# A hybrid NSA and Mamba2 block in float32: in the MLP, another order of the tiles in the first quad of each down projection, and the last split of squared rows one slot later

## The chip, the cores and the metric

The kernel runs on one core of one Trainium2 chip. The metric is the device time of one execution in microseconds (us), lower is better. The times of the kernel before are three runs; one more execution was recorded by the hardware profiler, and all rows and durations below come from that one.

## The reference, cut to what matters

One layer of a decoder block on 256 tokens of width 2048, all in float32: an RMSNorm, one wide input projection, two token mixers (sparse attention and a Mamba2 scan), gated and merged, an output projection, and then the MLP, which the change touches:

```python
h = h + merged @ w_out[l]
hn = rms_norm(h, norm_mlp_w[l])
h = h + jnp.square(jax.nn.relu(hn @ w_up[l])) @ w_down[l]      # w_up 2048 x 8192, w_down 8192 x 2048
return rms_norm(h, norm_final_w)
```

## The kernel before, in words

**One tile of weights.** All weights stream from HBM in tiles of 128 x 2 x 512 float32 (512 KB): two rows of blocks k = 2j and 2j + 1 of 512 columns. A tile takes four steps on four engines. SP loads it into one of four buffers `raw` (L674 in the MLP). ACT copies it, rounded, into one of four buffers `hi` (L1545, or L1541 for a tile of sums). DVE writes the remainder `lo = raw - hi` (L2132). PE multiplies the stationary activations, which are also kept as a high and a low part (`LAh`, `LAl`), with it: three matmuls of 512 columns for each product (high x high, high x low, low x high). Each engine has a program of its own in one common order of tiles, and they meet in counting semaphores: `s_lo` for `lo` tiles made, `s_mm` for tiles multiplied, `s_raw` for landings. Three limits follow. ACT may write `hi` of a tile only when PE is done with the tile four before. SP may load into a buffer only when DVE has made `lo` of the tile that was in it, which is four loads before. DVE and ACT work LEAD = 3 tiles ahead of the tile that PE is at: slot s of their program handles tile s + 3 of the phase and then runs the further work that is hooked to slot s.

**The MLP** has four phases, one for each 2048 of the 8192 hidden columns. A phase first makes its part of `hn @ w_up` in 4 chunks of 8 tiles (UP = 32 tiles), then multiplies the squared result with `w_down`, in two quads (QUAD = 22 tiles each, columns 0 to 1023 and 1024 to 2047). In the last phase the second quad is 16 plain tiles (TWO_ORDER) instead.

**The squared rows.** After chunk k of the up part is multiplied, slot 8k + 7 takes it out of PSUM (ACT L1527 and DVE L2100 with relu, ACT L1532 squares), DVE turns blocks of 32 x 32 (L423), and POOL spreads these over the partitions with four DMAs (L432, 128 KB each). Slot 8k + 11 then makes the stationary operands for k-blocks 4k to 4k + 3 of the down part: `LAh` on ACT (`act_split_s`, L447), which waits for the DMAs, and `LAl` on DVE (`dve_split_s`, L457), which waits for `LAh`. For k = 3 that is slot 35, when DVE has passed tile 38. PE needs these last rows only from the tile ("n", 0, 6) on.

**A quad** makes the output blocks of two column chunks for both halves of the tokens. Ten tiles are plain ("n"): j = 3 to 7 for each of the two chunks, 12 matmuls each. For j = 0 to 2 the kernel uses a scheme of seven block products in place of eight (`seven_products`), as four tiles each:

- a: weights of chunk 0, 6 matmuls. DVE first forms sums `TQ[0]` out of the raw tiles of a and b (L2122), so it waits until both have landed, then makes `lo`.
- b: weights of chunk 1, 3 matmuls. DVE forms `TQ[1]` in two steps with a drain between (L2126, L2128), then half a tile of `lo` (128 x 512).
- p and q: no load. ACT and DVE split `TQ[0]` and `TQ[1]`, 6 matmuls each.

The raw buffer of a is free again only when b's `lo` is made. So the load that goes into a's buffer and the one that goes into b's are both issued at that moment, four loads on. The order of the 22 tiles is QUAD_ORDER. `tiles_of_phase` turns it into the table that SP, ACT and DVE follow, and `four_blocks` on PE walks it too. In the words below a0, b0, p0, q0 are the tiles of j = 0, and n03 is ("n", 0, 3).

Of the kernel before, what the change touches and what calls it, by code (L numbers as in the profile page):

```python
# [76 lines left out]
G_MLP = 8 * C_MLP  # L77
G_END = G_MLP + 3 * PHASE + UP + QUAD + TWO

QUAD_ORDER = ([("n", 0, j) for j in (3, 4, 5)] + [("n", 1, 3)] + [(c, 0, 0) for c in "abpq"] +  # L80
              [("n", 1, j) for j in (4, 5)] + [(c, 0, 1) for c in "abpq"] + [("n", 0, j) for j in (6, 7)] +
              [(c, 0, 2) for c in "abpq"] + [("n", 1, j) for j in (6, 7)])
TWO_ORDER = [("n", c, j) for c in range(2) for j in range(8)]


def tiles_of_phase(last):

    tiles, loads = [("n", x // 8, x % 8, x) for x in range(UP)], UP
    for q in range(2):
        for kind, c, j in (TWO_ORDER if last and q else QUAD_ORDER):  # L90
            tiles.append((kind, 4 + 2 * q + (c if kind == "n" else 0), j, loads))
            loads += kind not in "pq"
    return tiles
# [25 lines left out]
def build(nc, a, out):  # L119
    ctx = ExitStack()  # L120
    with ctx:
# [16 lines left out]
        LAh = sb("LAh", [P, KT, S], F32R)  # L138
        LAl = sb("LAl", [P, KT, S], F32R)
# [303 lines left out]
        def act_split_s(act, n, Lh, k0, wc=None, later=0):  # L443

            act.wait_ge(s_sp[n % 2], 64 * (n // 2 + 1) + later)
            if wc is None:
                x = act.activation(tokens(Lh, k0), spread(n), ACT.Copy)  # L447
            else:
                for ct in range(4):
                    x = act.activation(tokens(Lh, k0 + ct, 1), spread(n, ct), ACT.Copy, scale=wc[:, ct:ct + 1])  # L450
            x.then_inc(s_tra, 2)

        def dve_split_s(dve, n, e, Lh, Ll, k0, wc=None):

            dve.wait_ge(s_tra, 2 * e + 2)
            if wc is None:
                x = dve.tensor_tensor(tokens(Ll, k0), spread(n), tokens(Lh, k0).bitcast(F32), ALU.subtract)  # L457
            else:
                for ct in range(4):
                    for t in range(2):  # L460
                        x = dve.scalar_tensor_tensor(tokens(Ll, k0 + ct, 1)[:, t, :, :], spread(n, ct)[:, t, :, :], wc[:, ct:ct + 1],
                                                     tokens(Lh, k0 + ct, 1)[:, t, :, :].bitcast(F32), ALU.mult, ALU.subtract)
            x.then_inc(s_trd, 1)
# [419 lines left out]
        def _(pe):  # L883
# [140 lines left out]
            for i in range(0, NG):  # L1024
                C, e = C_AT + 4 * i, E_AT + PER_AT * i
# [169 lines left out]
            def four_blocks(i, q):  # L1195

                g, C = G_MLP + PHASE * i + UP + QUAD * q, C_MLP + 8 * i + 4 + 2 * q
                p0, p1 = C % 2, (C + 1) % 2
                pe.wait_ge(s_acc, C - 1)
                for y, (kind, c, j) in enumerate(QUAD_ORDER):  # L1200
                    if kind == "a":
                        if j == 0:
                            pe.wait_ge(s_sfl, 2 * i + 2)
                            if 2 * i + q:
                                pe.wait_ge(s_ux, 2 * i + q)
                        seven_products(g + y, j, p0, p1)
                    elif kind == "n":
                        if c == 0 and j == 6:
                            pe.wait_ge(s_trd, E_MLP + 4 * i + 4)
                        if (c, j) == (1, 3):  # L1210
                            pe.wait_ge(s_acc, C)
                        mlp_group(g + y, (p0, p1)[c], j, LAh, LAl, t_first=(j == 3, j == 3), last=((c, j) == (1, 7)))
# [26 lines left out]
        def _(act):  # L1239
# [171 lines left out]
            for i in range(NG):  # L1411
                C, e = C_AT + 4 * i, E_AT + PER_AT * i
                hk, late = late, {}
# [11 lines left out]
                for r in range(4):  # L1425
                    n, s0 = 4 * i + r, SL_S[i][r]
# [81 lines left out]
            hk = scan_hooks(7, 12)  # L1508
# [67 lines left out]
            def mlp(i, first=False):  # L1576
                g, e = G_MLP + PHASE * i, E_MLP + 4 * i
                hk = {}
                for k in range(4):
                    hk[8 * k + 7] = [lambda k=k: first_rows(g + 8 * k + 8, (C_MLP + k) % 2), lambda k=k: square_rows(4 * i + k)]  # L1580
                    hk[8 * k + 11] = [lambda k=k: act_split_s(act, 8 + k, LAh, 4 * k, later=128 * i)]
                hk[14] = [lambda: row_sums(i)]
                hk[22] = [lambda: third_row_sums(i)]
                for q in range(1 if i == LAST else 2):
                    hk[UP + QUAD * q + 19] = [lambda q=q: copy_first(2 * i + q, g + UP + QUAD * q + 20)]
                if i == LAST:
                    hk[UP + QUAD + 3] = [lambda: act.wait_ge(s_hq, 7), lambda: residual_squares(C_END - 4, 0)]
                    hk[UP + QUAD + 4] = [lambda: act.wait_ge(s_ss, SS_WO + 2), lambda: residual_squares(C_END - 3, 1)]
                    hk[UP + QUAD + 7] = [lambda: act.wait_ge(s_ss, SS_WO + 4), lambda: residual_squares(C_END - 2, 2)]
                if first:  # L1590
                    hk[4] = [lambda: act_split_s(act, 7, LBh, 12, COLS[:, CN2 + 12:CN2 + 16])]
                phase_slots(i, hk)
# [22 lines left out]
        def _(dve):  # L1615
# [299 lines left out]
            for i in range(NG):  # L1915
                C, e = C_AT + 4 * i, E_AT + PER_AT * i
                hk, late = late, {}
# [14 lines left out]
                for r in range(4):  # L1932
                    n, s0 = 4 * i + r, SL_S[i][r]
# [14 lines left out]
            for i in range(2):  # L1948
                C = C_PA + 2 * i
                hk = {} if i else late  # L1950
# [107 lines left out]
            hk = scan_hooks(7, 12)  # L2058
# [165 lines left out]
            def mlp(i, before, first=False):  # L2224
                C, g, e = C_MLP + 8 * i, G_MLP + PHASE * i, E_MLP + 4 * i
                hk, late = before, {}
                for k in range(4):
                    hk[8 * k + 7] = [lambda k=k: mlp_rows(k, 4 * i + k, (C_MLP + k) % 2, XA_UP + 4 * i + k + 1)]
                    hk[8 * k + 11] = [lambda k=k: dve_split_s(dve, k, e + k, LAh, LAl, 4 * k)]
                hk[13] = [lambda: row_sums(i)]  # L2230
                hk[15] = hk.get(15, []) + [lambda: row_sums_low(i)]
                hk[21] = [third_row_sums]
                hk[24] = [lambda: third_row_sums_low(i)]
                quad_hooks(hk, late, i, 0)
                if i == LAST:
                    hk[UP + QUAD + 3] = [lambda: weigh(0), lambda: weigh(1)]
                    hk[UP + QUAD + 7] = [lambda: add_blocks(G_END - 8, C_END - 2, 2), lambda: weigh(2)]
                else:
                    quad_hooks(hk, late, i, 1)
                if first:  # L2240
                    hk[4] = [lambda: dve_split_s(dve, 7, E_WO + 3, LBh, LBl, 12, COLS[:, CN2 + 12:CN2 + 16])]
                phase_slots(i, hk)
                return late
# [62 lines left out]
```

## Time and profile before

| | |
|---|---|
| three runs | 2026.34 us median (2026.10 to 2029.11) |
| profiled execution, its own time | 2029.81 us |
| its span in the profile | 2028.1 us |
| PE busy | 2008.5 us, 99% |
| DVE, ACT, POOL busy | 1501.5 (74%), 1095.9 (54%), 277.9 us (14%) |
| share of the chain that ended last | PE 86%, DVE 6%, ACT 2%, DMA 2% |
| traffic | 203 GB/s mean |

The profile is one execution. Its busy times say how much of the span an engine worked, its rows of waits say how long an engine stood and for whom, and its timelines give the start of each instruction. "PEld" is the load of stationary weights, which overlaps the matmuls. A matmul's end is modelled, so of PE it is the starts that are read.

### The profile page before, as it was taken

How to read it: one execution, taken by the hardware profiler on the slowest of the kernel's cores; microseconds unless marked ns; L12 is line 12 of the kernel's file. 1: busy time of each engine (PE TensorE's matmuls, PEld its weight loads, DVE VectorE, ACT ScalarE, POOL GpSimd, SP SyncE). 2: the span in 40 equal slices, each digit the busy share in tenths (PEclk: the TensorE clock that was granted, in tenths of full speed). 3: DMA queues.
4: the chain of work that ended last, by engine and by line, in shares of the span. 5: the costliest groups of instructions: out<-in, count | busy, mean ns of one | idle time of the engine just before them, and what ended most of it. 6: DMA issues, size and time to landing. Idle time of an engine off the chain costs nothing.

```text
span 2028.1 us, 25969 instructions
## 1 busy us (share of the span) xinstructions
PE 2008.5 (99%) x9330; PEld 1655.7 (82%) x9330; DVE 1501.5 (74%) x1923; ACT 1095.9 (54%) x1533; POOL 277.9 (14%) x415
## 2 busy tenths in 40 slices
PE   9999999999999999999999999999999999999998
PEld 7888888888888888788888788888888888878886
DVE  5766868777765688886678877766886797697686
ACT  5444555555553576674567644555555554555554
POOL 4001111111010133331033310110000000100000
PEclk9999999999999999999999999999999999999999
DMA  8757666666657666666666677676666666666764
GB/s 259 222 173 216 194 190 197 189 196 191 183 181 229 186 193 191 195 195 209 177 186 197 192 237 244 215 222 216 199 210 215 197 211 203 215 200 203 230 206 150
DMA packets 203018, 411.52 MB, mean 203 GB/s; under 512 B 15296, under 2 KB 15648, under 8 KB 201488
## 3 DMA queue, kind: packets, MB, share of 16 engines
q1 hardware_dynamic: 188944, 364.75, 57.9%
q0 software_dynamic: 13776, 44.96, 7.7%
q8 instruction: 74, 1.21, 0.2%
q14 instruction: 48, 0.39, 0.1%
q10 hardware_dynamic: 176, 0.20, 0.0%
HBM read 379.91 MB, written 2.16 MB: 188 GB/s over the span
## 4 chain that ended last, share of the span: by engine, by line
PE 86%; DVE 6%; ACT 2%; DMA 2%; issue 1%; DVEq 1%; POOL 0%; ACTq 0%; POOLq 0%
PE acc L349 18%; PE acc L351 17%; PE acc L350 17%; PE acc L1155 8%; PE acc L1157 8%; PE acc L1156 8%; DVE lo L2132 2%; DVE lo L313 1%; DMA XTOK<-W 1%; PE x L1066 1%; PE tr L1015 1%; DMA raw<-w_in 1%; PE tr L384 1%; PE x L998 1%; ACT hi L307 1%
## 5 line engine op out<-in xcount | busy, mean ns | idle before, releaser
L313 DVE TENSOR_TENSOR lo<-raw,hi 128x1024 fp32r<-128x1024 f32 x434 | 532.2, 1240 | 267.5 <-ACT hi L307 260.9
L307 ACT ACTIVATE hi<-raw 128x1024 fp32r<-128x1024 f32 x434 | 452.1, 1057 | 329.8 <-PE acc L351 272.6
L349 PE MATMUL acc<-hi,LAh 128*128 128x512 f32 x1344 | 535.3, 398 | 3.2 <-DVE lo L313 2.8
L351 PE MATMUL acc<-hi,LAl 128*128 128x512 f32 x1344 | 524.3, 390 | 0.0
L350 PE MATMUL acc<-lo,LAh 128*128 128x512 f32 x1344 | 523.5, 390 | 0.0
L1545 ACT ACTIVATE hi<-raw 128x1024 fp32r<-128x1024 f32 x253 | 253.2, 1020 | 153.1 <-PE acc L1157 119.8
L2132 DVE TENSOR_TENSOR lo<-raw,hi 128x1024 fp32r<-128x1024 f32 x253 | 292.1, 1176 | 54.5 <-ACT hi L1545 51.6
L349 PEld LDWEIGHTS acc<-hi,LAh 128*128 128x128 f32 x1344 | 252.3, 188 | 58.8 <-issue 7.6
L351 PEld LDWEIGHTS acc<-hi,LAl 128*128 128x128 f32 x1344 | 252.2, 188 | 54.1
L350 PEld LDWEIGHTS acc<-lo,LAh 128*128 128x128 f32 x1344 | 252.5, 188 | 51.2 <-issue 1.4
L1155 PE MATMUL acc<-hi,LBh 128*128 128x512 f32 x512 | 199.2, 389 | 0.0
L1156 PE MATMUL acc<-lo,LBh 128*128 128x512 f32 x512 | 199.2, 389 | 0.0
L1157 PE MATMUL acc<-hi,LBl 128*128 128x512 f32 x512 | 199.2, 389 | 0.0
L349 PE MATMUL acc<-hi,LBh 128*128 128x512 f32 x384 | 150.4, 392 | 0.0
L351 PE MATMUL acc<-hi,LBl 128*128 128x512 f32 x384 | 149.5, 389 | 0.0
L350 PE MATMUL acc<-lo,LBh 128*128 128x512 f32 x384 | 149.4, 389 | 0.0
L1155 PE MATMUL acc<-hi,LAh 128*128 128x512 f32 x328 | 127.6, 389 | 0.0
L1156 PE MATMUL acc<-lo,LAh 128*128 128x512 f32 x328 | 127.6, 389 | 0.0
L1157 PE MATMUL acc<-hi,LAl 128*128 128x512 f32 x328 | 127.6, 389 | 0.0
L1157 PEld LDWEIGHTS acc<-hi,LBl 128*128 128x128 f32 x512 | 96.1, 188 | 20.1
L1156 PEld LDWEIGHTS acc<-lo,LBh 128*128 128x128 f32 x512 | 96.1, 188 | 20.0
L1155 PEld LDWEIGHTS acc<-hi,LBh 128*128 128x128 f32 x512 | 96.1, 188 | 19.7
(423 smaller groups left out, 2475.0 us busy)
## 6 DMA issues: line engine op xcount, KB each, us to landing
raw<-w_in SPq DMA_DIRECT2D x304, 512.0 KB, 4.3
raw<-w_up SPq DMA_DIRECT2D x128, 512.0 KB, 4.1
raw<-w_down SPq DMA_DIRECT2D x128, 512.0 KB, 4.9
raw<-w_proj_ssm SPq DMA_DIRECT2D x64, 512.0 KB, 4.4
raw<-w_proj_nsa SPq DMA_DIRECT2D x32, 512.0 KB, 4.7
raw<-w_out SPq DMA_DIRECT2D x32, 512.0 KB, 5.4
W<-acs_rows POOLq DMA_DIRECT2D x8, 1024.0 KB, 6.6
W<-TB POOLq DMA_DIRECT2D x48, 128.0 KB, 4.3
```

The costliest lines, as they stand in the source:

```text
L307: act.activation(hi[:, sl, :, :], raw[:, sl, :, :], ACT.Copy).then_inc(s_hi, 1)
L313: dve.tensor_tensor(lo[:, sl, :, :], raw[:, sl, :, :], hi[:, sl, :, :].bitcast(F32), ALU.subtract).then_inc(s_lo, 1)
L349: pe.matmul(o, xh, wh, start=(k == 0), stop=False)
L350: pe.matmul(o, xh, wl, start=False, stop=False)
L351: x = pe.matmul(o, xl, wh, start=False, stop=(k == KT - 1))
L384: x = pe.transpose((banks or TR)[b][:, (ct % 2) * S + t * P:(ct % 2) * S + (t + 1) * P], src[:, t, ct * P:(ct + 1) * P], identf[:, :])
L998: pe.matmul(X6[:, :], Q[:, n, P:S], K[:, :, 0:2 * P].rearrange("p k (b n) -> p b k n", b=2), start=(p_ == 0), stop=(p_ == 2), skip_group_c ...
L1155: pe.matmul(o, xh, wh, start=(kk == 0 and t_first[t]), stop=False)
L1156: pe.matmul(o, xh, wl, start=False, stop=False)
L1157: x = pe.matmul(o, xl, wh, start=False, stop=(last and kk == 1))
L1545: act.activation(hi[:, sl, k0:2, :], raw[:, d % RING, k0:2, :], ACT.Copy).then_inc(s_hi, 1)
L2132: dve.tensor_tensor(lo[:, sl, k0:2, :], src, hi[:, sl, k0:2, :].bitcast(F32), ALU.subtract).then_inc(s_lo, 1)
```

## The change

The first quad of every phase gets an order of its own: six plain tiles first instead of four, and one plain tile between the groups of four instead of two. The second quad keeps its order. The last split of squared rows (k = 3) moves from slot 35 to slot 36 on ACT and on DVE, in all four phases.

```diff
-QUAD_ORDER = ([("n", 0, j) for j in (3, 4, 5)] + [("n", 1, 3)] + [(c, 0, 0) for c in "abpq"] +
-              [("n", 1, j) for j in (4, 5)] + [(c, 0, 1) for c in "abpq"] + [("n", 0, j) for j in (6, 7)] +
-              [(c, 0, 2) for c in "abpq"] + [("n", 1, j) for j in (6, 7)])
+QUAD_ORDER = (([("n", c, j) for c in range(2) for j in (3, 4, 5)] + [(c, 0, 0) for c in "abpq"] + [("n", 0, 6)] +
+               [(c, 0, 1) for c in "abpq"] + [("n", 0, 7)] + [(c, 0, 2) for c in "abpq"] + [("n", 1, j) for j in (6, 7)]),
+              ([("n", 0, j) for j in (3, 4, 5)] + [("n", 1, 3)] + [(c, 0, 0) for c in "abpq"] +
+               [("n", 1, j) for j in (4, 5)] + [(c, 0, 1) for c in "abpq"] + [("n", 0, j) for j in (6, 7)] +
+               [(c, 0, 2) for c in "abpq"] + [("n", 1, j) for j in (6, 7)]))
...
-        for kind, c, j in (TWO_ORDER if last and q else QUAD_ORDER):
+        for kind, c, j in (TWO_ORDER if last and q else QUAD_ORDER[q]):
...
-                for y, (kind, c, j) in enumerate(QUAD_ORDER):
+                for y, (kind, c, j) in enumerate(QUAD_ORDER[q]):
...
-                    hk[8 * k + 11] = [lambda k=k: act_split_s(act, 8 + k, LAh, 4 * k, later=128 * i)]
+                    hk[8 * k + 11 + k // 3] = [lambda k=k: act_split_s(act, 8 + k, LAh, 4 * k, later=128 * i)]
...
-                    hk[8 * k + 11] = [lambda k=k: dve_split_s(dve, k, e + k, LAh, LAl, 4 * k)]
+                    hk[8 * k + 11 + k // 3] = [lambda k=k: dve_split_s(dve, k, e + k, LAh, LAl, 4 * k)]
```

On DVE, in the first phase, from the take of the last up chunk (`XR<-acc`) through the first group of four to the second. Before (the rows `lo<-TQ` are p and q, `lo<-raw` of 128x512 is b):

```order
L2100 TENSOR_SCALAR XR<-acc,RS 128x512
L423 STREAM_TRANSPOSE W<-Y 128x4x4x32 x2
L2132 TENSOR_TENSOR lo<-raw,hi 128x1024
L2122 TENSOR_TENSOR TQ<-raw 128x1024
L2132 TENSOR_TENSOR lo<-raw,hi 128x1024
L2126 TENSOR_TENSOR TQ<-TQ,raw 128x512
L2128 TENSOR_TENSOR TQ<-raw,TQ 128x512
L2132 TENSOR_TENSOR lo<-raw,hi 128x512
L2132 TENSOR_TENSOR lo<-TQ,hi 128x1024
L457 TENSOR_TENSOR LAl<-XTOK,LAh 128x1024
L2132 TENSOR_TENSOR lo<-TQ,hi 128x1024
L2132 TENSOR_TENSOR lo<-raw,hi 128x1024 x2
```

The same place with the change (line numbers are two higher):

```order
L2102 TENSOR_SCALAR XR<-acc,RS 128x512
L425 STREAM_TRANSPOSE W<-Y 128x4x4x32 x2
L2134 TENSOR_TENSOR lo<-raw,hi 128x1024 x3
L2124 TENSOR_TENSOR TQ<-raw 128x1024
L2134 TENSOR_TENSOR lo<-raw,hi 128x1024
L2128 TENSOR_TENSOR TQ<-TQ,raw 128x512
L2130 TENSOR_TENSOR TQ<-raw,TQ 128x512
L2134 TENSOR_TENSOR lo<-raw,hi 128x512
L459 TENSOR_TENSOR LAl<-XTOK,LAh 128x1024
L2134 TENSOR_TENSOR lo<-TQ,hi 128x1024 x2
L2134 TENSOR_TENSOR lo<-raw,hi 128x1024
```

Two plain tiles have moved ahead of the first sums, `LAl` stands before both p0 and q0 instead of between them, and one plain tile is left before the next sums. On ACT, at the same place, before:

```order
L1532 ACTIVATE Y<-XR 128x1024
L1545 ACTIVATE hi<-raw 128x1024 x2
L1545 ACTIVATE hi<-raw 128x512
L1541 ACTIVATE hi<-TQ 128x1024
L447 ACTIVATE LAh<-XTOK 128x1024
L1541 ACTIVATE hi<-TQ 128x1024
L1545 ACTIVATE hi<-raw 128x1024 x3
```

and with the change:

```order
L1534 ACTIVATE Y<-XR 128x1024
L1547 ACTIVATE hi<-raw 128x1024 x4
L1547 ACTIVATE hi<-raw 128x512
L449 ACTIVATE LAh<-XTOK 128x1024
L1543 ACTIVATE hi<-TQ 128x1024 x2
L1547 ACTIVATE hi<-raw 128x1024 x2
```

`LAh` now stands before both high parts of the sums. No instruction is added or removed on any engine.

## Rows read from the trace of the kernel before

**Rows 1.** The page, parts 1 and 6: busy times and loads.
```profile
PE 2008.5 (99%) x9330; PEld 1655.7 (82%) x9330; DVE 1501.5 (74%) x1923; ACT 1095.9 (54%) x1533; POOL 277.9 (14%) x415
...
raw<-w_down SPq DMA_DIRECT2D x128, 512.0 KB, 4.9
```

**Rows 2.** Waits of PE and PEld: total us, times, longest us.
```profile
PE tr L1170 <- DVE lo L2132: 3.9, 4, 1.2
...
PEld x L1170 <- DVE lo L2132: 1.7, 3, 0.6
```

**Rows 3.** Timeline of PE, first phase: start us, us, engine, line.
```profile
1417.91 0.39 PE L1155 MATMUL acc<-hi,LAh 128*128 128x512 f32 x1
...
1420.63 0.39 PE L1155 MATMUL acc<-hi,LAh 128*128 128x512 f32 x1
...
1431.96 0.39 PE L1172 MATMUL x<-hi,LSl 128*128 128x512 f32 x1
1433.51 0.50 PE L1170 MATMUL tr<-hi,LSh 128*128 128x512 f32 x1 [1.16 <-DVE lo L2132]
1433.85 0.40 PE L1171 MATMUL tr<-lo,LSh 128*128 128x512 f32 x1
```

**Rows 4.** Timeline of ACT, first quad of the first phase.
```profile
1430.00 1.06 ACT L447 ACTIVATE LAh<-XTOK 128x1024 fp32r<-128x1024 f32 x1 [2.67 <-DMA XTOK<-W]
```

**Rows 5.** Timeline of DVE, first quad of the first phase.
```profile
1422.80 1.18 DVE L2132 TENSOR_TENSOR lo<-raw,hi 128x1024 fp32r<-128x1024 f32 x1
1423.89 1.22 DVE L2122 TENSOR_TENSOR TQ<-raw 128x1024 f32<-128x1024 f32 x1
...
1426.17 0.68 DVE L2126 TENSOR_TENSOR TQ<-TQ,raw 128x512 f32<-128x512 f32 x1
...
1427.53 0.69 DVE L2132 TENSOR_TENSOR lo<-raw,hi 128x512 fp32r<-128x512 f32 x1
1428.14 1.22 DVE L2132 TENSOR_TENSOR lo<-TQ,hi 128x1024 fp32r<-128x1024 f32 x1
1431.10 1.23 DVE L457 TENSOR_TENSOR LAl<-XTOK,LAh 128x1024 fp32r<-128x1024 f32 x1 [1.74 <-ACT LAh L447]
1432.24 1.22 DVE L2132 TENSOR_TENSOR lo<-TQ,hi 128x1024 fp32r<-128x1024 f32 x1
```

**Rows 6.** Line L674, the loads issued at 1424.0 and 1767.7: time to landing.
```profile
L674 SPq DMA_DIRECT2D raw<-w_down x1: 368/368/368, 1424.0 to 1424.0; - x1
...
DMA to landing us min/median/max: 5.6/5.6/5.6
...
L674 SPq DMA_DIRECT2D raw<-w_down x1: 367/367/367, 1767.7 to 1767.7; - x1
...
DMA to landing us min/median/max: 5.3/5.3/5.3
```

**Rows 7.** The same for the loads at 1440.0 and 1440.4, released by b1.
```profile
L674 SPq DMA_DIRECT2D raw<-w_down x2: 367/418/468, 1440.0 to 1440.4; - x2
...
DMA to landing us min/median/max: 4.2/4.6/5.0
```

**Rows 8.** The same for the load at 1449.9, released by b2.
```profile
L674 SPq DMA_DIRECT2D raw<-w_down x1: 367/367/367, 1449.9 to 1449.9; - x1
...
DMA to landing us min/median/max: 4.0/4.0/4.0
```

**Rows 9.** Busy time from 1453.3 to 1474.1: PE, PEld, DVE, ACT, POOL, clock, DMA.
```profile
1453.30:1474.10 20.80, 20.62 (x91) 16.73 (x90) 20.06 (x24) 10.30 (x11) 0.00 (x0) 1.00 0.61 194
```

**Rows 10.** Timeline of DVE, into the second quad.
```profile
1453.30 3.50 DVE L2132 TENSOR_TENSOR lo<-raw,hi 128x1024 fp32r<-128x1024 f32 x3
...
1472.83 2.36 DVE L2132 TENSOR_TENSOR lo<-TQ,hi 128x1024 fp32r<-128x1024 f32 x2
```

**Rows 11.** Timeline of PE, second quad.
```profile
1473.53 0.39 PE L1172 MATMUL acc<-hi,LSl 128*128 128x512 f32 x1
1474.11 0.50 PE L1170 MATMUL x<-hi,LSh 128*128 128x512 f32 x1 [0.18 <-DVE lo L2132]
```

## The prediction

> **What bounds the kernel.** I read the page first: PE is busy for 99% of the span [rows 1], in the stretch in question at a granted clock of 1.00, the higher of its two levels (2.4 GHz) [rows 9]. So no order of work can win more than the few microseconds in which PE stands. Then the waits of PE, to see where it stands in the MLP: four waits at the first matmul of a q tile (3.9 us by PE) and three at a p tile (by PEld), all for DVE's `lo` [rows 2]. Then the timeline of PE, whose starts give the real cost. The pace is 0.227 us a matmul: a plain tile of 12 takes 1420.63 - 1417.91 = 2.72 us [rows 3], so a, p and q (6 matmuls) take 1.36 and b (3) 0.68, a group of four 4.76. In the first phase q0 starts 1.55 us after the matmul before it, and its second matmul 0.34 after the first: 1.32 + 0.11 = 1.43 us lost [rows 3]. By PE's modelled ends the four are 1.0 us of idle each on average [rows 2]; with the 0.2 us more that the starts show and the 0.1 of the slow matmul after it, the four come to 5.0 us. In the second quad p0 starts 0.58 us after the matmul before it [rows 11], a loss of 0.35 + 0.1 = 0.45 us, and over three phases some 1.3 us. **All that PE loses in the MLP is 6.3 us.**
>
> The timeline of DVE says why. At slot 35 `LAl` waits for `LAh` (1.74 us of idle) [rows 5], and `LAh` had waited 2.67 us for the spread's DMA [rows 4]. The `lo` of q0 stands behind it in DVE's order and starts at 1432.24, when PE has been waiting since 1432.19.
>
> **What the change removes.** `LAh` becomes ready at 1431.1 by the DMA [rows 4], and the six plain tiles now keep PE busy until 1417.91 + 6 x 2.72 = 1434.23, when a0 starts (it was 1428.79). q0 is needed at 1434.23 + 1.36 + 0.68 + 1.36 = 1437.63, over 5 us after `LAl` could be done. The wait at q0 for the squared rows goes: 5.0 us. If nothing else moved, that would be the result.
>
> **What it costs: the loads behind the sums.** The sums of a need both raw tiles. DVE spends on a and b, by the starts from 1423.89 to 1428.14 in [rows 5], 2 x 1.14 for the sums and a's `lo`, 1.36 for b's two steps and 0.61 for b's `lo`, 4.25 us, and on p and q 1.14 each, 6.5 us against PE's 4.76: DVE falls back 1.8 us in a group and wins 2.72 - 1.14 = 1.58 in a plain tile. With two plain tiles between groups it catches up, with one it does not. Worse is the loop through SP: b's `lo` releases the buffer, the load of the next b is issued, lands, and only then can the next sums start. From b's `lo` to b's `lo` that is 4.0 us of load (4.2 for the first of a pair, 4.0 alone [rows 7, 8]), 0.1 to start, and 4.33 us on DVE (4.25, with the whole 0.69 of b's `lo`): **8.4 us**. PE's period was 4.76 + 2 x 2.72 = 10.2 and becomes 4.76 + 2.72 = **7.5 us**. So each step of the new order loses 0.9 us of whatever lead DVE has. Two steps, four phases.
>
> How large is the lead? b0 is now load number 8 of the quad, so it goes into the buffer of n13 and is issued when that `lo` is made, at 1424.0; that load took 5.6 us, and 5.3 in the third phase [rows 6]. It sat in front of a plain tile before and nobody minded. Now the sums of a0 start at 1429.7 instead of 1423.89. I walk it on, each start from the last by the steps above:
>
> - b0's `lo` 1433.3 to 1434.0, `LAl` 1433.95, p0's `lo` 1435.1 to 1436.3 (PE wants it at 1436.27: no slack), q0's to 1437.45 (1437.63), n06's to 1438.6.
> - The load of b1 is issued at 1434.05 and lands at 1438.05, before DVE is free. Sums of a1 at 1438.5, `lo` of b1 1442.15 to 1442.85, of p1 to 1444.0. PE wants p1 at 1443.75: **0.3 us** lost with the slow first matmul.
> - The load of b2 is issued at 1442.9 and lands at 1446.9. DVE is free at 1446.1 and stands 0.9 us. Sums of a2 at 1447.0, `lo` of b2 to 1451.35. PE wants b2 at 1450.55 + 0.3: **0.5 us** lost. p2's `lo` comes to 1452.45, PE wants it at 1452.0: **0.5 us** lost.
>
> That is 1.3 us in the first phase against 1.43 before; with the 0.1 to 0.3 us shorter first load of the others about 1.15. In all 4.75 us against 5.0: **-0.3 us**. The stall is not gone, it moves from q0 to p1, b2 and p2.
>
> **What comes behind it.** b2's `lo` ends at 1451.3; it was 1449.9 [rows 8], when the load of the next quad's first tile was issued. With 4.0 us that tile lands at 1455.3, ACT takes 1.1, and its `lo` starts at 1456.4; it was third in the block at 1453.30, 1455.5 [rows 10]. From there to p0 of the second quad DVE has no reserve: 20.06 us busy in 20.8 [rows 9]. So p0's `lo`, which ended at 1472.83 + 1.22 = 1474.05 [rows 10], ends 0.9 us later, while PE arrives at nearly the old time (its loss in the first quad is 0.1 us smaller). The loss there grows from 0.45 by 0.95 to 1.4 us. The second quad of three phases is of this kind: **+2.9 us**. The last phase has plain tiles there and a longer lead, so nothing.
>
> **The sum:** -0.3 + 2.9 = +2.6 us on the profiled execution's own 2029.81 us. That one is 3.5 us above the median of the runs shown, so I put the sum on the median: 2026.34 + 2.7 = **2029.0 us**. Two tenths of a per cent are 4.05 us here, about what a measurement of this kernel can tell from no change. No DMA, matmul or evacuation is added, and SP's loads keep their number; in the changed order SP waits on the same counter. ACT has `LAh` ahead of p0's and q0's high parts, but it ends at 1431.3, and p0's can't start before PE is done with the tile four before, n14, at 1417.91 + 5 x 2.72 + 0.2 = 1431.7 (0.2 us is what the last matmul takes beyond the start of the next).
>
> **The unknown cost** is the landing of b1, b2 and n03 of the next quad in the new traffic. From below, I take 3.8 us, 0.2 under [rows 8], since the 4.0 and 4.2 of [rows 7, 8] differ by as much. It takes 0.2 us from each of two loops and from the second quad: some -2 us on the whole. From above, 5.0 us as the second of a pair [rows 7] adds a microsecond to both loops, about +9 us. I take 4.0 to 4.1, because each of these loads is the first issued for over 4 us, like the one of [rows 8].
>
> At this point the Trainium skill ("DMA: Bandwidth & Descriptors", section "Anatomy of one DMA") gives a transfer a fixed cost of some 2.0 us plus its bytes at 436 GB/s. That makes an estimate of 3.2 us for 512 KB, by which the loops would take 7.6 us, the first quad would lose nothing and the second about 0.8 us, 4 us faster in all. The rows have 4.0 to 5.6 us for that size, so by measurement the loops don't close, and the sum goes by them.
>
> **The rivals.**
>
> - *Faster, the loads keep up.* If the sums' loads land in 3.8 us or less in the quieter traffic, and the first b's load in 4 instead of 5.6 (the spread's four DMAs go at that time, and it is now followed by two more loads), p1, b2 and p2 cost under 0.1 us each. Then the first quad's 5.0 us goes and the second quad's loss grows to some 0.8 us: -4 to -5 us, 2022 us. For it: DVE's work alone, 6.5 + 1.14 = 7.65 us, is within 0.2 us of PE's period. Against: not one load after a b tile in the rows shown is under 4.0. The page's rule above would make this case. Chance 0.14.
> - *Slower than forecast: the loads behind b are later.* At 4.4 to 4.6 us each, a1 and a2 are late too. The first quad then costs 1.9 to 2.2 us, the second 1.8: -6.3 + 8.2 + 5.4 = +6 to +8 us, 2033 us. It decides from 4.2 us on. For it: the median of all loads of `w_down` is 4.9 us [rows 1], and three loads now go within 2.5 us at the head of the quad. Chance 0.31.
> - *The change doesn't do what it says:* `LAh` could be pushed by later spread DMAs beyond 1433.9, so that `LAl` waits again before both p0 and q0. It needs 3 us more than the 1430.0 of [rows 4]. It would add 1 us or more a phase, and I count it into the case above.
>
> **How the numbers follow.** The forecast (a change of -1 to +4 us, within 0.2%) has 0.55, faster 0.14, slower 0.31. The range goes from 2023.5 (most of the faster case is left out) to 2034.5 (the far half of the slower case is left out): 8 in 10.
>
> **What would show it.** No wait of PE at q0 (`tr L1170`). In its place waits at `x L1170` (p1), `acc L1170` (b2) and p2 in the first quad, 0.2 to 0.6 us each, none at a0, b0. DVE idle before the sums of a2 (L2124) for `raw<-w_down`, some 0.9 us, and before those of a0 over 3 us. The waits at p0 of the second quad at 1.2 to 1.5 us instead of 0.5. I am wrong if PE shows no wait in the first quad, if the loads behind b land in clearly other than 4.0 us, or if the second quad's wait stays at 0.5 us.

## Result and profile after

| | median | lowest to highest | runs |
|---|---|---|---|
| before | 2026.98 us | 2024.51 to 2031.11 | 22 |
| changed | 2030.65 us | 2026.65 to 2033.96 | 22 |

The ratio is 1.0016, 95% interval 1.0010 to 1.0022: the changed kernel is 2.0 to 4.5 us slower, 3.2 us in the middle. The forecast was +2.7 us and "within 0.2%". Single runs of either kernel spread over 7 us, and the profiled execution of the changed kernel (2029.28 us) happens to be shorter than that of before (2029.81). So what the change does is read from PE inside the MLP, not from the two spans. The first and the last matmul of the MLP, before:

```profile
1330.87 0.39 PE L1155 MATMUL acc<-hi,LBh 128*128 128x512 f32 x1
...
2019.19 0.39 PE L363 MATMUL acc<-hi,LAl 128*128 128x512 f32 x1
```

and changed:

```profile
1326.90 0.39 PE L1157 MATMUL acc<-hi,LBh 128*128 128x512 f32 x1
...
2018.61 0.39 PE L365 MATMUL acc<-hi,LAl 128*128 128x512 f32 x1
```

The MLP takes 688.3 us before and 691.7 changed, 3.4 us more. The changed execution reached it 4.0 us earlier, after work that is the same in both, and from the last matmul to the end both take 8.9 us. That is why its span came out shorter.

Page of the changed kernel (its line numbers are two higher in the stage in question), parts 1 and 4, in answer to [rows 1], and the share of the chain that ended last:

```profile
PE 2009.9 (99%) x9330; PEld 1654.2 (82%) x9330; DVE 1500.0 (74%) x1923; ACT 1096.2 (54%) x1533; POOL 276.8 (14%) x415
...
PE 83%; DVE 8%; DMA 3%; issue 2%; ACT 2%; DVEq 1%; POOL 1%; ACTq 0%; POOLq 0%
```

All work is the same; the chain runs 3 points less over PE and more over DVE and the loads. The waits of PE and of its weight loads, in answer to [rows 2] (total us, times, longest):

```profile
PE x L1172 <- DVE lo L2134: 4.2, 7, 1.2
...
PE acc L1172 <- DVE lo L2134: 0.6, 2, 0.3
...
PEld x L1172 <- DVE lo L2134: 9.5, 14, 1.6
```

The four waits at q0 (`tr`, 3.9 us) are gone. In their place stand waits at p tiles (`x`) and at b tiles (`acc`). The timeline of PE shows them in the first phase, where the first quad begins at 1413.94: p0 and, in the third group, b2 and p2, then p0 of the second quad. It answers to [rows 3] and [rows 11].

```profile
1432.07 0.39 PE L1174 MATMUL acc<-hi,LSl 128*128 128x512 f32 x1
1432.41 0.50 PE L1172 MATMUL x<-hi,LSh 128*128 128x512 f32 x1
...
1446.81 0.40 PE L1174 MATMUL acc<-hi,LAl 128*128 128x512 f32 x1
1447.52 0.51 PE L1172 MATMUL acc<-hi,LSh 128*128 128x512 f32 x1 [0.31 <-DVE lo L2134]
1447.86 0.40 PE L1173 MATMUL acc<-lo,LSh 128*128 128x512 f32 x1
1448.10 0.40 PE L1174 MATMUL acc<-hi,LSl 128*128 128x512 f32 x1
1448.65 0.50 PE L1172 MATMUL x<-hi,LSh 128*128 128x512 f32 x1 [0.16 <-DVE lo L2134]
...
1469.65 0.39 PE L1174 MATMUL acc<-hi,LSl 128*128 128x512 f32 x1
1471.19 0.50 PE L1172 MATMUL x<-hi,LSh 128*128 128x512 f32 x1 [1.16 <-DVE lo L2134]
1471.53 0.40 PE L1173 MATMUL x<-lo,LSh 128*128 128x512 f32 x1
```

From start to start, less the pace of 0.227 us and with the slow matmul behind each gap, p0 costs 0.2 us, p1 0.15, b2 0.6, p2 0.4, and p0 of the second quad 1.54 - 0.23 + 0.11 = 1.4 us. The same reading in all phases gives

| us lost by PE | phase 1 | phase 2 | phase 3 | phase 4 | sum |
|---|---|---|---|---|---|
| first quad, before | 1.44 | 1.31 | 1.10 | 1.19 | 5.0 |
| first quad, changed | 1.43 | 1.11 | 1.18 | 1.28 | 5.0 |
| second quad, before | 0.46 | 0.40 | 0.40 | 0 | 1.3 |
| second quad, changed | 1.43 | 1.49 | 1.46 | 0 | 4.4 |

6.3 us before, 9.4 changed. The first quads lose about what they lost before, in other places (from its first matmul to that of the second quad the first one takes 42.93 us before and 43.01 changed, by 1417.91 and 1460.84, 1413.94 and 1456.95), and the second quads lose 3.1 us more.

DVE in the first quad of the first phase, in answer to [rows 5]:

```profile
1418.83 3.47 DVE L2134 TENSOR_TENSOR lo<-raw,hi 128x1024 fp32r<-128x1024 f32 x3
1425.76 1.22 DVE L2124 TENSOR_TENSOR TQ<-raw 128x1024 f32<-128x1024 f32 x1 [3.46 <-DMA raw<-w_down]
...
1430.01 1.22 DVE L459 TENSOR_TENSOR LAl<-XTOK,LAh 128x1024 fp32r<-128x1024 f32 x1
1431.14 2.35 DVE L2134 TENSOR_TENSOR lo<-TQ,hi 128x1024 fp32r<-128x1024 f32 x2
1433.41 1.22 DVE L2134 TENSOR_TENSOR lo<-raw,hi 128x1024 fp32r<-128x1024 f32 x1
1434.55 1.22 DVE L2124 TENSOR_TENSOR TQ<-raw 128x1024 f32<-128x1024 f32 x1
...
1438.18 0.68 DVE L2134 TENSOR_TENSOR lo<-raw,hi 128x512 fp32r<-128x512 f32 x1
...
1443.14 1.23 DVE L2124 TENSOR_TENSOR TQ<-raw 128x1024 f32<-128x1024 f32 x1 [0.86 <-DMA raw<-w_down]
...
1446.78 0.68 DVE L2134 TENSOR_TENSOR lo<-raw,hi 128x512 fp32r<-128x512 f32 x1
```

Two waits for loads are new: 3.46 us before the sums of a0, 0.86 us before those of a2. `LAl` of the last squared rows no longer waits, in any phase. The loads behind it (line L676, issued behind n13's, b1's and b2's `lo`), in answer to [rows 6 to 8]:

```profile
L676 SPq DMA_DIRECT2D raw<-w_down x1: 368/368/368, 1420.1 to 1420.1; - x1
DMA to landing us min/median/max: 5.6/5.6/5.6
...
L676 SPq DMA_DIRECT2D raw<-w_down x1: 368/368/368, 1438.9 to 1438.9; - x1
DMA to landing us min/median/max: 4.1/4.1/4.1
...
L676 SPq DMA_DIRECT2D raw<-w_down x1: 368/368/368, 1447.5 to 1447.5; - x1
DMA to landing us min/median/max: 4.1/4.1/4.1
```

b1's load, issued behind b0's `lo` at 1430.1, took 4.2 us. Over the four phases b1's took 4.1 to 4.4, b2's 3.8 to 4.2 and that of the next quad's first tile 4.1 to 4.2 us.

The measured 4.1 to 5.6 us decide, and the loop does not close. The Trainium skill's figures ("DMA: Bandwidth & Descriptors", "Anatomy of one DMA — SWDGE (gpsimd) path") give 3.2 us for 512 KB by estimate, and by it the kernel would have become faster. But that section fits them to DMAs issued by GpSimd, and these loads are issued by SP; the prediction did not say so.

At the head of the second quad ACT and then DVE stand for the load that b2's `lo` released (the first tile of the quad, n03):

```profile
1451.63 1.06 ACT L1547 ACTIVATE hi<-raw 128x1024 fp32r<-128x1024 f32 x1 [1.72 <-DMA raw<-w_down]
```

```profile
1452.72 1.23 DVE L2134 TENSOR_TENSOR lo<-raw,hi 128x1024 fp32r<-128x1024 f32 x1 [0.72 <-ACT hi L1547]
```

### The profile page after: what moved, and what is told of

It reads as the page before. It is cut to its first block, busy times and chain, and to the rows that moved or that the text cites. A ratio compares the mean times of both kernels' runs of the same rounds, so it can differ in the third digit from the quotient of the medians.

```text
span 2027.5 us, 25969 instructions
## 1 busy us (share of the span) xinstructions
PE 2009.9 (99%) x9330; PEld 1654.2 (82%) x9330; DVE 1500.0 (74%) x1923; ACT 1096.2 (54%) x1533; POOL 276.8 (14%) x415
## 4 chain that ended last, share of the span: by engine, by line
PE 83%; DVE 8%; DMA 3%; issue 2%; ACT 2%; DVEq 1%; POOL 1%; ACTq 0%; POOLq 0%
PE acc L351 18%; PE acc L353 18%; PE acc L352 18%; PE acc L1159 7%; PE acc L1157 7%; PE acc L1158 7%; DVE lo L2134 3%; DMA raw<-w_down 2%; DVE TQ L2124 1%; PE x L1068 1%; PE tr L1017 1%; DVE lo L315 1%; PE x L1000 1%; PE tr L386 1%; DVE TQ L2130 1%
## 5 line engine op out<-in xcount | busy, mean ns | idle before, releaser
L315 DVE TENSOR_TENSOR lo<-raw,hi 128x1024 fp32r<-128x1024 f32 x434 | 532.0, 1240 | 267.6 <-ACT hi L309 260.7
L309 ACT ACTIVATE hi<-raw 128x1024 fp32r<-128x1024 f32 x434 | 452.3, 1057 | 331.4 <-PE acc L353 267.1
L1547 ACT ACTIVATE hi<-raw 128x1024 fp32r<-128x1024 f32 (+1 forms) x253 | 254.0, 1021 | 178.1 <-PE acc L1159 126.3
L2134 DVE TENSOR_TENSOR lo<-raw,hi 128x1024 fp32r<-128x1024 f32 (+1 forms) x253 | 292.1, 1173 | 57.8 <-ACT hi L1547 56.1
```

What stands on the lines that cost most here:

```text
L309: act.activation(hi[:, sl, :, :], raw[:, sl, :, :], ACT.Copy).then_inc(s_hi, 1)
L315: dve.tensor_tensor(lo[:, sl, :, :], raw[:, sl, :, :], hi[:, sl, :, :].bitcast(F32), ALU.subtract).then_inc(s_lo, 1)
L1547: act.activation(hi[:, sl, k0:2, :], raw[:, d % RING, k0:2, :], ACT.Copy).then_inc(s_hi, 1)
L2134: dve.tensor_tensor(lo[:, sl, k0:2, :], src, hi[:, sl, k0:2, :].bitcast(F32), ALU.subtract).then_inc(s_lo, 1)
```

## Experiments

"Loss" is what PE loses in the MLP of the profiled execution, read as in the table above. "MLP" is the time from the first to the last start of its matmuls in the same execution. e2 ran 5 times and e5 7 times, the others 10 or 11.

| kernel | plain tiles ahead of each group of four, first / second quad | split at slot | loss us | MLP us | ratio of times (95%) |
|---|---|---|---|---|---|
| before | 4, 2, 2 / 4, 2, 2 | 35 | 6.3 | 688.3 | 1 |
| changed | 6, 1, 1 / 4, 2, 2 | 36 | 9.4 | 691.7 | 1.0016 (1.0010 to 1.0022) |
| e1, e8 | 4, 2, 2 / 4, 2, 2 | 36 | 2.0, 2.3 | 684.1, 684.3 | 0.9990 (0.9981 to 0.9999), 0.9980 (0.9971 to 0.9989) |
| e2 | 6, 1, 1 / 4, 2, 2 | 35 | 15.8 | 698.3 | 1.0050 (1.0036 to 1.0064) |
| e3 | changed, b loads halved | 36 | 6.8 | 689.0 | 1.0009 (1.0000 to 1.0018) |
| e4 | 5, 1, 2 / 5, 2, 1 | 36 | 0.5 | 682.5 | 0.9977 (0.9968 to 0.9987) |
| e5 | 4, 2, 2 / 5, 2, 1 | 37 | 0 | 682.0 | 0.9969 (0.9958 to 0.9981) |
| e6 | 6, 1, 1 / 5, 2, 1 | 36 | 3.7 | 686.0 | 0.9999 (0.9990 to 1.0009) |
| e7 | 5, 1, 2 / 4, 2, 2 | 36 | 3.6 | 685.7 | 0.9981 (0.9971 to 0.9990) |
| e9 | changed, shorter b | 36 | 5.6 | 687.7 | 0.9997 (0.9988 to 1.0007) |

In every row the MLP takes 682.0 us and the loss, within 0.5 us. The rest of an execution has the same code in all kernels and moves by itself: the MLP began between 1326.4 and 1330.9 us, and 8.9 us followed its last matmul each time. So the loss is the firmer measure of the two.

The plain tiles keep their own order everywhere (n03, n04, n05, n13, n14, n15, n06, n07, and n16, n17 last); only where the groups of four cut in differs.

### e1 and e8: the later split alone

```diff
-                    hk[8 * k + 11] = [lambda k=k: act_split_s(act, 8 + k, LAh, 4 * k, later=128 * i)]
+                    hk[8 * k + 11 + k // 3] = [lambda k=k: act_split_s(act, 8 + k, LAh, 4 * k, later=128 * i)]
...
-                    hk[8 * k + 11] = [lambda k=k: dve_split_s(dve, k, e + k, LAh, LAl, 4 * k)]
+                    hk[8 * k + 11 + k // 3] = [lambda k=k: dve_split_s(dve, k, e + k, LAh, LAl, 4 * k)]
```

> The quads keep the order of the kernel before, only the last split of squared rows goes to slot 36. Theory A (what stood at q0 was the lo of q0 behind LAl, and the new loss comes from the order of the tiles, through the loads behind b): the wait of PE at q0 goes in all four phases, at most 0.2 us is left at q0 or the plain tile behind it, the second quad keeps its 0.4 to 0.45 us at p0, so PE loses some 2 us in the MLP in place of 6.3, and the time is 4 to 5 us under the kernel before (ratio 0.998). Rival B (the later split itself delays ACT and DVE, and that is what costs in the changed kernel): PE loses at the plain tiles behind q0 or in the second quad, and the time is equal to or above the kernel before.

The loss is 2.0 us: 0.2 in each first quad and 0.4 in each of three second quads, as theory A had it. The 0.2 us stand at the plain tile behind q0, whose `lo` now comes behind `LAl`. DVE in the first quad:

```profile
1425.89 1.22 DVE L2143 TENSOR_TENSOR lo<-TQ,hi 128x1024 fp32r<-128x1024 f32 x1
1427.84 1.23 DVE L2143 TENSOR_TENSOR lo<-TQ,hi 128x1024 fp32r<-128x1024 f32 x1 [0.73 <-ACT hi L1552]
1428.98 1.22 DVE L468 TENSOR_TENSOR LAl<-XTOK,LAh 128x1024 fp32r<-128x1024 f32 x1
```

The `lo` of q0 now stands in front of `LAl` and is on time. The time fell by 0.1% where 0.2% was expected, so the same kernel went again:

> The split alone at slot 36 once more, to settle its size: PE lost 4.3 us less in the MLP, but the time fell by only 0.1% (interval 0.01 to 0.19%). If the loss of PE in the MLP is the whole effect (theory A), the two sets of runs together give a ratio near 0.998. If the later split costs something outside the MLP's matmuls (rival B), they stay at 0.999 or above.

Loss 2.3 us, ratio 0.998. The two intervals overlap between 0.9981 and 0.9989, 2 to 4 us, while 4.0 to 4.3 us were lost less. The ratios alone don't tell the two apart, since their mean of 0.9985 lies between the 0.998 and 0.999 that the expectation gave. The traces do: the MLP is 4.2 and 4.0 us shorter than before, and what stands behind it took the same 8.9 us. A cost outside the MLP would have to lie ahead of it, where the code is the same. So rival B falls by the traces. **The one-slot shift is good by itself; the order costs more than the shift gives.**

### e2: the order without the later split

The changed kernel, with the slot as it was, on both engines:

```diff
-                    hk[8 * k + 11 + k // 3] = [lambda k=k: dve_split_s(dve, k, e + k, LAh, LAl, 4 * k)]
+                    hk[8 * k + 11] = [lambda k=k: dve_split_s(dve, k, e + k, LAh, LAl, 4 * k)]
```

> The first quad has the changed order, but the split stays at slot 35, ahead of b0's lo. Theory A (the loop from b's lo through the load of the next b): with the split in front of b0's lo the load of b1 is issued 1.1 us later, and the second group of four is late as well. PE loses 0.4 to 0.6 us each at b1, p1, b2 and p2, 1.9 to 2.2 us in the first quad (1.3 in the changed kernel), and still 1.4 us in the second. The sum in the MLP is 12 to 13 us, the time 5 to 7 us above the kernel before (ratio 1.003). Rival B (the split's slot doesn't matter in the new order, since the squared rows are there in time anyway): the same as the changed kernel, some 3 us above before, ratio 1.0015.

It is the slowest of all: 15.8 us lost, 10 us more time. Theory A had the sign and the places, and the size too small (12 to 13 us). PE at the second group, b1 and p1:

```profile
1435.31 0.39 PE L1183 MATMUL acc<-hi,LAl 128*128 128x512 f32 x1
1436.10 0.50 PE L1181 MATMUL acc<-hi,LSh 128*128 128x512 f32 x1 [0.39 <-DVE lo L2143]
...
1437.23 0.50 PE L1181 MATMUL x<-hi,LSh 128*128 128x512 f32 x1 [0.17 <-DVE lo L2143]
```

In three phases the first quad loses 2.8 to 3.3 us, in the second phase 2.0. `LAl` in front of b0's `lo` holds back the load of b1, so the sums of a1 wait 0.69 to 1.16 us for it, and all that follows is late by as much. Rival B (slot 35 or 36 is the same) falls. The parts don't add: the shift alone takes 4 us of loss away and the order alone adds 9.5, but the two together add 3.1, since in the new order the slot decides when b1's load is issued.

### e3: half the bytes for b

```diff
+                    if kind == "b" and x < UP + QUAD:
+                        sp.dma_start(raw[:, d % RING, 0, :], src[:, 0, :]).then_inc(s_raw[d % RING], 16)
+                    else:
...
```

> The changed kernel, but in the first quad of each phase the loads of the b tiles bring only the first of their two blocks of rows (256 KB in place of 512), and the second block is what the buffer held; nothing else changes, all sums, splits and matmuls are done. Theory A (the load behind b bounds the loop): the load lands 0.5 to 0.8 us sooner, DVE's idle time before the sums of a2 (0.9 us) goes down to 0.1 to 0.3, and PE loses at most 0.3 us in the first quad in place of 1.3 and 0.7 to 0.9 us at p0 of the second in place of 1.4. The time is at or under the kernel before. Rival C (DVE's own work per group, 7.65 us against PE's 7.5, is what bounds, the load only fills the same time): PE loses 1.0 us or more in the first quad and 1.3 or more in the second as in the changed kernel, and the time stays 3 us above before.

The loads of b in the first phase landed in 4.9, 3.9 and 3.5 us instead of 5.6, 4.2 and 4.1; half the bytes save only 0.3 to 0.7 us. DVE before the sums of a2:

```profile
1445.13 1.22 DVE L2136 TENSOR_TENSOR TQ<-raw 128x1024 f32<-128x1024 f32 x1 [0.22 <-DMA raw<-w_down]
```

That wait went from 0.86 to 0.22 us, and the first quad's losses to 0.35, 0.39, 1.14 and 0.56 us. In the third phase the loads were hardly faster (3.44 and 0.57 us of idle), and there the loss stayed. So the loads of the b tiles carry most of the first quad's loss. The second half of the expectation fell: the second quads still lost 1.4 to 1.5 us, as rival C had it. The expectation overlooked PE. In the first phase the sums of a2 came 1.1 us earlier in the quad, and PE, which lost 1.1 us less, came as much earlier too, so that DVE was no nearer to it. The time (ratio 1.0000 to 1.0018) did not come at or under the kernel before either, which agrees with a loss of 6.8 against 6.3 us.

### e4: five plain tiles first

Against the changed kernel, in the first order; the second is five, two, one (its diff stands with e5):

```diff
-QUAD_ORDER = (([("n", c, j) for c in range(2) for j in (3, 4, 5)] + [(c, 0, 0) for c in "abpq"] + [("n", 0, 6)] +
-               [(c, 0, 1) for c in "abpq"] + [("n", 0, 7)] + [(c, 0, 2) for c in "abpq"] + [("n", 1, j) for j in (6, 7)]),
+QUAD_ORDER = (([("n", 0, 3), ("n", 0, 4), ("n", 0, 5), ("n", 1, 3), ("n", 1, 4)] +
+               [(c, 0, 0) for c in "abpq"] +
+               [("n", 1, 5)] +
+               [(c, 0, 1) for c in "abpq"] +
+               [("n", 0, 6), ("n", 0, 7)] +
...
```

> Split at slot 36; first quad with five plain tiles first, one after the first group of four and two after the second; second quad with five first, two after the first group and one after the second. Theory A (each short gap costs 0.9 us of DVE's lead, and a lead of 1 us or more is there if the short gap comes where the lead is large): no wait of PE above 0.2 us in any quad, 0 to 1.5 us lost in the MLP, the time 5 to 6 us under the kernel before (ratio 0.997). Rival D (any gap of one plain tile makes PE wait, wherever it is): 0.5 us or more lost at the group behind the single tile in each quad, 3.5 us or more in the MLP, and the time within 3 us of before.

0.5 us lost in all. DVE does wait for loads here (0.78 to 1.06 us before the sums of a2), but with lead enough that PE feels none of it. Rival D falls, for a single plain tile behind b0 or behind b1 did not make PE wait in itself.

### e5: the shift to slot 37, and another second quad

The first order is that of the kernel before. Against e1, in the second order and in both engines' splits:

```diff
-              ([("n", 0, 3), ("n", 0, 4), ("n", 0, 5), ("n", 1, 3)] +
+              ([("n", 0, 3), ("n", 0, 4), ("n", 0, 5), ("n", 1, 3), ("n", 1, 4)] +
                [(c, 0, 0) for c in "abpq"] +
-               [("n", 1, 4), ("n", 1, 5)] +
+               [("n", 1, 5), ("n", 0, 6)] +
                [(c, 0, 1) for c in "abpq"] +
-               [("n", 0, 6), ("n", 0, 7)] +
+               [("n", 0, 7)] +
...
-                    hk[8 * k + 11 + k // 3] = [lambda k=k: dve_split_s(dve, k, e + k, LAh, LAl, 4 * k)]
+                    hk[8 * k + 11 + k // 3 * 2] = [lambda k=k: dve_split_s(dve, k, e + k, LAh, LAl, 4 * k)]
```

> First quad in the order of the kernel before (gaps of 4, 2 and 2 plain tiles), the last split at slot 37, behind q0's lo; second quad with gaps of 5, 2 and 1. Theory A: the split is behind everything that PE wants at that time, so q0 costs nothing; the longer start of the second quad takes its wait at p0 away. PE loses 0 to 0.6 us in the MLP and the time is 4 to 6 us under the kernel before (ratio 0.9975), within noise the same as the kernel with 5, 1, 2. Rival D (a gap of one plain tile makes PE wait wherever it is): 0.5 us or more in each second quad at its third group.

**PE loses nothing in the MLP.** No two of its 3009 matmuls start more than 0.25 us apart. DVE at q0 and after:

```profile
1423.69 1.22 DVE L2143 TENSOR_TENSOR lo<-TQ,hi 128x1024 fp32r<-128x1024 f32 x1
1425.64 1.23 DVE L2143 TENSOR_TENSOR lo<-TQ,hi 128x1024 fp32r<-128x1024 f32 x1 [0.73 <-ACT hi L1552]
1427.00 1.22 DVE L2143 TENSOR_TENSOR lo<-raw,hi 128x1024 fp32r<-128x1024 f32 x1
1428.14 1.22 DVE L468 TENSOR_TENSOR LAl<-XTOK,LAh 128x1024 fp32r<-128x1024 f32 x1
```

Median 2021.09 us, ratio 0.9969 (0.9958 to 0.9981), 4 to 8.5 us under the kernel before: the 6.3 us that were lost there. It beats both kernels. Two things were changed at once, but they act at different places: slot 37 takes away the 0.2 us of e1 in each first quad, and the longer start the 0.4 us in each second quad.

### e6: the changed first quad with a longer start of the second

The changed kernel, with the second order alone edited:

```diff
-              ([("n", 0, j) for j in (3, 4, 5)] + [("n", 1, 3)] + [(c, 0, 0) for c in "abpq"] +
-               [("n", 1, j) for j in (4, 5)] + [(c, 0, 1) for c in "abpq"] + [("n", 0, j) for j in (6, 7)] +
+              ([("n", 0, 3), ("n", 0, 4), ("n", 0, 5), ("n", 1, 3), ("n", 1, 4)] +
+               [(c, 0, 0) for c in "abpq"] +
+               [("n", 1, 5), ("n", 0, 6)] +
+               [(c, 0, 1) for c in "abpq"] +
+               [("n", 0, 7)] +
...
```

> The changed kernel's first quad (6, 1, 1, split at slot 36) with a second quad of 5, 2 and 1. Theory A (the second quad's 1.4 us come from DVE's short lead when it enters it, and that lead is used up by p0): the first quad still loses 1.0 to 1.4 us in every phase, but p0 of the second, which now comes 2.7 us later for PE and 1.1 us later for DVE, is no longer late; 0 to 0.5 us remain in each second quad. 5 to 7 us lost in the MLP in place of 9.3, the time within 2 us of the kernel before. Rival E (the second quad's loss is its own and does not depend on the gap ahead of p0): 1.0 us or more in each second quad.

The second quads lost 0, 0.27 and 0.24 us, so rival E falls. The first quads lost 0.9, 0.64, 1.0 and 0.68, less than the 1.0 to 1.4 expected, though their code is that of the changed kernel: in this execution DVE waited 0.38 to 0.42 us before the sums of a2, in the changed kernel's 0.56 to 0.98. A load that is 0.3 us later or earlier moves the loss by about as much, and single executions differ by that. The loss of 3.7 us in all is under the 5 to 7 expected. The time (2.0 us under to 1.8 over before) is somewhat above what this loss says, though the MLP of the profiled execution is 2.3 us shorter than before; that stays open.

### e7: a first quad without loss before the old second quad

The first order of e4, the second of the kernel before. Against e4:

```diff
-              ([("n", 0, 3), ("n", 0, 4), ("n", 0, 5), ("n", 1, 3), ("n", 1, 4)] +
+              ([("n", 0, 3), ("n", 0, 4), ("n", 0, 5), ("n", 1, 3)] +
                [(c, 0, 0) for c in "abpq"] +
-               [("n", 1, 5), ("n", 0, 6)] +
+               [("n", 1, 4), ("n", 1, 5)] +
                [(c, 0, 1) for c in "abpq"] +
-               [("n", 0, 7)] +
+               [("n", 0, 6), ("n", 0, 7)] +
...
```

> First quad with gaps of 5, 1 and 2 plain tiles and the split at slot 36, second quad in the order of the kernel before. Theory A: no loss in the first quad, as in the kernel with both orders new, but DVE enters the second quad with 0.4 us less lead over PE than in the kernel before (4.87 against 5.27 us at its first tile), so p0 there costs 0.45 + 0.4 = 0.8 to 0.9 us in three phases. 2.4 to 2.9 us lost in the MLP, the time 3 to 4 us under the kernel before. Rival F (the second quad's loss grows only with losses in the first, not with the lead): 0.45 us at most there, 1.3 us in all.

The first quads lost 0, 0, 0.26 and 0 us, the second quads 0.75, 1.1 and 1.53. Rival F falls: the loss in the second quad can grow where the first loses nothing. But it varied over the phases more than the 0.8 to 0.9 expected. DVE stood 0.72, 1.09 and 1.73 us before the sums of a2 in these phases, for b2's loads of 4.7, 5.1 and 5.7 us, and the loss grew with it. The table below shows what it follows.

### e9: a shorter b on DVE

```diff
-                    dve.tensor_tensor(TQ[:, 1, 0, :], TQ[:, 0, 1, :], raw[:, sa, 0, :], ALU.add)
-                    dve.drain()
+                    if c >= 6 or i == 0:
+                        dve.tensor_tensor(TQ[:, 1, 0, :], TQ[:, 0, 1, :], raw[:, sa, 0, :], ALU.add)
+                        dve.drain()
```

> The changed kernel, but in the first quad of phases 2 to 4 DVE leaves out the first of b's two steps and its drain (L2126 of the kernel before; TQ[1, 0] is what an earlier quad left there), 0.75 us less of DVE in each group of four, with all loads as in the changed kernel. The first phase is unchanged and serves as its own comparison. Theory A (each step of the loop from b's lo through the load to the next b's lo is 0.75 us shorter, 7.7 us against PE's 7.5, and what the second quad loses is set by how early b2's lo is made ahead of PE): the first quad loses 0.9 to 1.4 us in phase 1 and 0 to 0.2 us in phases 2 to 4; b2's lo is 2.2 us earlier, of which PE takes back 1.2, so DVE enters the second quad 1 us further ahead and p0's loss there falls from 1.45 to 0.4 to 0.6 us in phases 2 and 3, and stays at 1.4 in phase 1. Rival G (the second quad's loss after the changed first quad has another cause, such as later loads, since it stayed at 1.4 us when b's loads were halved): it stays at 1.2 us or more in phases 2 and 3 too.

The first quad lost 1.38 us in phase 1, where nothing is left out, and **0 in phases 2 to 4**. That is the loop made 0.75 us shorter. The second quads, though, still lost 1.26 and 1.46 us. Taken alone that speaks for rival G. DVE at the head of the second quad in phase 2, whose first quad began at 1589.00:

```profile
1625.72 1.23 DVE L2144 TENSOR_TENSOR lo<-raw,hi 128x1024 fp32r<-128x1024 f32 x1 [0.42 <-ACT hi L1556]
1627.04 1.29 DVE L2180 TENSOR_TENSOR BCT<-acc,BCT 128x512 f32<-128x512 f32 x2
1628.24 1.22 DVE L2144 TENSOR_TENSOR lo<-raw,hi 128x1024 fp32r<-128x1024 f32 x1
1629.90 0.69 DVE L2187 TENSOR_TENSOR BCT<-tr,BCT 128x512 f32<-128x512 f32 x1 [0.44 <-issue]
...
1636.13 1.22 DVE L2133 TENSOR_TENSOR TQ<-raw 128x1024 f32<-128x1024 f32 x1
```

In phase 2 b2's `lo` was 1.8 us earlier in the quad than in the changed kernel, not 2.2, since the sums of a2 still waited 0.2 us for the load. PE came 1.1 us earlier too, for it lost nothing in the first quad. And DVE stood 0.44 us for no releaser that the profile shows, so that DVE won 0.2 us of lead in place of the 0.65 that these two figures leave. In phase 3 b2's load took 4.6 us (3.9 in the changed kernel) and the sums of a2 waited 0.77 us; b2's `lo` came 1.2 us earlier, PE 1.2 us too, and no lead was won. So DVE was hardly nearer to PE than before, and the question is whether that distance is what counts.

### One measure for all second quads

Take the start of the sums of a0 in the second quad (L2124 in the changed kernel) less the start of the first matmul of that quad on PE. In the first phase, before:

```profile
1460.84 0.39 PE L1155 MATMUL acc<-hi,LAh 128*128 128x512 f32 x1
```

```profile
1465.69 1.22 DVE L2122 TENSOR_TENSOR TQ<-raw 128x1024 f32<-128x1024 f32 x1
```

and changed:

```profile
1456.95 0.39 PE L1157 MATMUL acc<-hi,LAh 128*128 128x512 f32 x1
...
1462.78 1.22 DVE L2124 TENSOR_TENSOR TQ<-raw 128x1024 f32<-128x1024 f32 x1
```

By these rows the lag is 4.85 us before and 5.83 changed. All kernels that have the old order in the second quad, read the same way, three phases each:

| kernel | lag, us | loss of PE at p0, us | loss in the first quad ahead |
|---|---|---|---|
| before | 4.85, 4.80, 4.79 | 0.46, 0.40, 0.40 | 1.44, 1.31, 1.10 |
| e1 | 4.79, 4.80, 4.80 | 0.40, 0.40, 0.41 | 0.20, 0.20, 0.20 |
| e8 | 4.79, 5.03, 4.85 | 0.40, 0.64, 0.46 | 0.19, 0.19, 0.19 |
| e7 | 5.15, 5.50, 5.91 | 0.75, 1.10, 1.53 | 0, 0, 0.26 |
| e9 | 5.92, 5.65, 5.85 | 1.54, 1.26, 1.46 | 1.38, 0, 0 |
| e3 | 5.77, 5.92, 5.85 | 1.38, 1.53, 1.47 | 0.35, 0.39, 1.14 |
| changed | 5.83, 5.89, 5.86 | 1.43, 1.49, 1.46 | 1.43, 1.11, 1.18 |
| e2 | 6.02, 5.86, 5.80 | 1.63, 1.47, 1.41 | 3.30, 2.04, 3.19 |

**The loss is the lag less 4.4 us**, within 0.02 us in all 24 cases, whatever the first quad lost. The 4.4 us are an account and no second cause: from these sums to the end of p0's `lo` DVE works 8.4 us without a wait (1465.69 to 1474.05 before), while PE has 12.95 us of matmuls from the quad's start to p0 (four plain tiles, a0 and b0); the last 0.2 us of the difference are p0's start and the slow matmul behind it. So all that a change ahead can do to p0 is to move the lag. The stretch of the changed kernel from 1449.3 to 1471.0 shows how little reserve there is (busy time of PE, PEld, DVE, ACT, POOL, then clock, DMA share and GB/s): DVE is busy 20.24 of 21.7 us, and its one wait is the 0.72 us for the first tile of the quad.

```profile
1449.30:1471.00 21.70, 20.73 (x92) 16.83 (x90) 20.24 (x24) 10.66 (x12) 0.00 (x0) 1.00 0.63 201
```

That answers rival G in part. The second quad's loss has the cause of theory A, but the lag can stay where b's loop is short, since it counts against a PE that also came earlier. In phase 3 of e9 and in e3 these two account for it; the 0.44 us of e9's phase 2 stays open.

## Why the prediction was right

- **What is removed.** "The wait at q0 for the squared rows goes: 5.0 us." It went in all four phases. e1 shows that the shift by one slot does this without the new order, at 0.2 us.
- **The late load of b0.** The walk put the sums of a0 11.8 us behind the first matmul of the quad (1429.7 - 1417.91). They came at 1425.76 - 1413.94 = 11.8. DVE stood 3.46 us there, "over 3 us" forecast.
- **The loop.** Sums of a1 at 20.6 us and of a2 at 29.1 us in the walk; 20.6 and 29.2 in the trace. The idle time before a2's was to be 0.9 and was 0.86 us in the first phase, 0.56 to 0.98 over the four. The loads of b1, b2 and the next quad landed in 4.2, 4.1 and 4.1 us, where 4.0 to 4.1 was taken. The prediction called the load of [rows 8] alone; another was issued 0.4 us behind it (1450.3, landed in 4.9 us). The size holds all the same, for the three loads are each the first of such a pair. e3 and e9 shortened the loop at its two ends, the load and DVE, and each time the first quad's loss went down or away.
- **The first quad.** Forecast 4.75 us of loss against 5.0, measured 5.0 against 5.0. In the first phase 0 at p0, 0.3 at p1, 0.5 at b2 and 0.5 at p2 were forecast; it was 0.2, 0.15, 0.6 and 0.4. So the total is better than its parts, whose errors of 0.1 to 0.2 us cancel by luck. The sums in the other phases were 1.1 to 1.3 us, forecast "about 1.15".
- **The second quad.** Forecast 1.4 us each, +2.9 in all; measured 1.43 to 1.49, +3.1 in all. The walk had DVE 0.9 us later by the load behind b2, and it was 1.1 later.
- **The sum.** +2.6 us forecast on the profiled execution, +3.1 in PE's gaps, +3.4 in the length of the MLP, +3.2 (2.0 to 4.5) in the times. The half microsecond that is missing between the forecast and the gaps is the 0.3 us that the first quads didn't win and 0.2 in the second.
- **The rivals.** Faster needed landings of 3.8 us or less behind b. Such landings were there in the second phase (3.8 behind b1), and the loss of that phase was the smallest of the four, 1.1 us, but one load is not enough. Slower needed 4.4 us and more for each, which came once among the eight loads of b1 and b2 (b1's in the second phase, 4.4). That `LAh` could be late again did not happen: `LAl` of the last squared rows waited in no phase.

What the prediction had not weighed is that the two parts of the change could be told apart: it summed them, and so did not say that PE would lose 4 us less by the shift alone and 9.5 more by the order alone.

## What to carry to other kernels

When an engine's wait is caused by one instruction in front of the one that matters, move that instruction behind it first (e1), before the order of the tiles is touched: the order also decides when buffers come free, and so when loads are issued. Before two groups are moved closer, compare the period of the bound engine with the whole loop through the buffer: release, load, landing, and the work up to the next release. And follow the lead of the feeding engine across the border into the next stage, as here all that PE lost more appeared there, in work that the change didn't touch.

## What the runs showed of the hardware that was not expected

- Halving a load from 512 to 256 KB shortened its time to landing in the first phase only from 5.6, 4.2 and 4.1 to 4.9, 3.9 and 3.5 us, and hardly in the third (5.5, 4.1 and 3.9 against 5.6, 3.8 and 3.8).
- The same load at the same place varies over phases and executions enough to move the result: DVE's idle time before the sums of a2 was 0.56 to 0.98 us in the changed kernel and 0.38 to 0.42 in e6, whose first quad has the same program. In e7 it was 0.72, 1.09, 1.73 and 0.86 us over the four phases. Why was not tried.
- In the changed kernel's first quads, of two loads issued 0.4 us apart the first took 3.8 to 4.4 us and the second 4.8 to 5.3 (in the first phase 4.2 and 5.1, 4.1 and 4.9, 4.1 and 4.9).
- The load of b0, issued while the four spread DMAs of POOL run and followed by two more loads within 2.3 us, took 5.3 to 5.6 us. Whether the spread is the reason was not tried.
